# A hybrid encoder trunk in fp32 on one core: another order in the opening, in cross attention's second pair, and for the residual's transposes

## What is computed

```python
h = x + concat([y_a, y_b, y_c]) @ w_out
h = h + cross_attention(rmsnorm(h, norm_cross), rmsnorm(mem, norm_mem), wq, wkv, wo)

def cross_attention(u, m, wq, wkv, wo):          # 4 heads of 128
    q = (u @ wq).reshape(bsz, seq, 4, 128)
    kv = (m @ wkv).reshape(bsz, mlen, 2, 4, 128)
    k, v = kv[:, :, 0], kv[:, :, 1]
    s = einsum('bshd,bmhd->bhsm', q, k) * 128 ** -0.5
    p = softmax(s, axis=-1)
    o = einsum('bhsm,bmhd->bshd', p, v).reshape(bsz, seq, 512)
    return o @ wo
```

## Time and profile before

| | |
|---|---|
| time, median of 3 runs | 1197.31 us (1195.26, 1197.31, 1197.39) |
| profiled execution | 1195.13 us |
| its span (first to last instruction) | 1193.3 us, mean granted clock 0.997 |
| outside the span | 1.8 us |
| PE busy | 98% of the span |
| DVE, ACT busy | 75%, 55% |
| HBM | 181 GB/s over the span |

### The profile page before, as it was taken

The page is one execution under the profiler, slowest core; times in us unless marked ns, Lnnn a source line. Parts: engine busy times, 40 slices in busy tenths (PEclk is TensorE's granted clock), DMA queues, the critical chain, the costliest instruction groups (busy, mean ns, idle before and its releaser), DMA issues.

```text
span 1193.3 us, 18816 instructions
## 1 busy us (share of the span) xinstructions
PE 1171.8 (98%) x6956; PEld 1039.8 (87%) x6956; DVE 893.7 (75%) x1271; ACT 658.4 (55%) x870; POOL 0.2 (0%) x4
## 2 busy tenths in 40 slices
PE   8999999999999999999999999999999999999996
PEld 8899999999887978888888888888888888888885
DVE  6775999778866767877777777777677777777777
ACT  6555665566744557555455545454564645555455
POOL 0000000000000000000000000000000000000000
PEclk9999999999999999999999999999999999999999
DMA  9766656434556455675756657585766567575751
GB/s 352 215 162 177 177 142 177 133 108 141 200 194 180 155 164 139 204 212 176 210 177 195 192 164 199 167 222 185 195 192 189 176 195 192 174 211 176 212 176 71
DMA packets 303214, 217.11 MB, mean 182 GB/s; under 512 B 11350, under 2 KB 263998, under 8 KB 302526
## 3 DMA queue, kind: packets, MB, share of 16 engines
q1 hardware_dynamic: 302990, 216.31, 61.8%
q10 hardware_dynamic: 176, 0.14, 0.1%
HBM read 214.33 MB, written 2.10 MB: 181 GB/s over the span
## 4 chain that ended last, share of the span: by engine, by line
PE 86%; DVE 7%; issue 2%; ACT 1%; SPq 1%; DMA 1%; ACTq 0%; DVEq 0%
PE bank L1392 27%; PE bank L1396 14%; PE bank L1366 10%; PE bank L1367 9%; PE bank L1368 9%; PE bank L1369 4%; PE bank L1370 4%; PE bank L1371 4%; DVE lo L798 2%; DMA raw<-in_cross_wkv_dram 1%; PE bank L1464 1%; PE bank L1495 1%; ACT hi L388 1%; DVE arena L1000 1%; PE bank L1428 1%
## 5 line engine op out<-in xcount | busy, mean ns | idle before, releaser
L798 DVE TENSOR_TENSOR lo<-raw,hi 128x2048 fp32r<-128x2048 f32 x195 | 446.3, 2289 | 128.8 <-ACT hi L388 118.9
L388 ACT CAST hi<-raw 128x2048 fp32r<-128x2048 f32 x195 | 371.6, 1911 | 104.8 <-PE bank L1368 98.4
L1392 PE MATMUL bank<-ux,hi 128*128 128x512 f32 x1408 | 336.5, 391 | 0.0
L1392 PEld LDWEIGHTS bank<-ux,hi 128*128 128x128 f32 x1408 | 259.1, 188 | 50.6 <-DVE arena L1293 0.2
L1396 PEld LDWEIGHTS bank<-ux,lo 128*128 128x128 f32 x1408 | 180.9, 191 | 7.1
L1396 PE MATMUL bank<-ux,lo 128*128 128x256 f32 x1408 | 183.1, 283 | 0.0
L1366 PE MATMUL bank<-hi,ch 128*128 128x512 f32 x464 | 181.4, 391 | 1.4 <-DVE cl L1232 1.4
L1367 PE MATMUL bank<-lo,ch 128*128 128x512 f32 x464 | 180.3, 388 | 0.0
L1368 PE MATMUL bank<-hi,cl 128*128 128x512 f32 x464 | 180.2, 388 | 0.0
L1369 PE MATMUL bank<-ux,hi 128*128 128x256 f32 (+1 forms) x592 | 170.9, 289 | 0.0
L1371 PE MATMUL bank<-ux,lo 128*128 128x256 f32 (+1 forms) x592 | 168.1, 284 | 0.0
(11 more groups left out here) (247 smaller groups left out, 969.9 us busy)
## 6 DMA issues: line engine op xcount, KB each, us to landing
raw<-in_ffn_w_up_dram SPq DMA_DIRECT2D x88, 1024.0 KB, 5.8
raw<-in_ffn_w_down_dram SPq DMA_DIRECT2D x44, 1024.0 KB, 5.1
raw<-in_w_in_dram SPq DMA_DIRECT2D x28, 1024.0 KB, 5.6
raw<-in_w_out_dram SPq DMA_DIRECT2D x16, 1024.0 KB, 5.1
raw<-in_cross_wkv_dram SPq DMA_DIRECT2D x7, 1024.0 KB, 10.0
arena<-in_x_dram SPq DMA_DIRECT2D x4, 1024.0 KB, 8.2
raw<-in_cross_wq_dram SPq DMA_DIRECT2D x4, 1024.0 KB, 5.4
raw<-in_cross_wo_dram SPq DMA_DIRECT2D x4, 1024.0 KB, 5.1
```

The costliest lines, as they stand in the source:

```text
L388: a.mark(act.copy(hi[:, n % RING, :], raw[:, n % RING, :]), S("hi_ready"))
L798: d.mark(dve.tensor_tensor(lo[:, n % RING, :], raw[:, n % RING, :], hi[:, n % RING, :].bitcast(F32), ALU.subtract), S("lo_ready"))
L1392: pe.matmul(bank[b][:, :], hi[:, s, k * P:(k + 1) * P], ux[:, k, :, :].rearrange("p a b -> p (a b)"), start=(k == 0), stop=False)
```

## The change

It leaves the number of matmuls, transposes, copies, subtractions and DMAs as it is, and the order of the DMAs.

1. Opening, PE: the 48 matmuls of a quarter are no longer taken tile by tile in threes, but in passes over several tiles: first hi x `uh`, which waits only for `hi_ready` and `mem_hi`; later the passes that need a low part. Chunk 0 goes in two halves, and the transposes of quarter 1 lie between them; the transposes of quarters 2 and 3 lie behind the first pass of chunks 1 and 2. The same for the value products (`value_rows`): the 8 matmuls hi x `uh` wait for `hi_ready` alone.
2. Opening, ACT and DVE: group 0 of `mem` ahead of the first half of chunk 0, `split(1)` ahead of the groups 2 and 3, `split(4)` behind the squares of x, on ACT `split(5)` ahead of x's scaling, on DVE `split(5)` behind `key_taken`.
3. Output projection: the first 12 matmuls of chunk n + 1 go ahead of `turn_block`.
4. Cross attention: blocks 0 and 1 of `cross_wo` go both ahead of `turn_probs`, and the first two k tiles of block 2 (chunk `N_WO + 2`) around `head_out`: 4 matmuls before it, 8 behind it. So `split(N_WO + 2)` moves forward: on ACT ahead of the exponentials of the second pair, on DVE behind its divisions and ahead of `cross_lo(1)`.

```diff
@@ ACT
+            token_hi("mem", 0, V_MEM, mem_bank(0))
             act.wait_ge(S("first_landed").sem, 16)
             a.mark(act.copy(hi[:, 0, 0:CH // 2], raw[:, 0, 0:CH // 2]), S("first_hi"))
-            for g in (0, 1):
-                token_hi("mem", g, V_MEM, mem_bank(g))
+            token_hi("mem", 1, V_MEM, mem_bank(1))
             act.wait_ge(S("raw_landed0").sem, 16)
             a.mark(act.copy(hi[:, 0, CH // 2:], raw[:, 0, CH // 2:]), S("hi_ready"))
+            split(1)
             for g in (2, 3):
                 token_hi("mem", g, V_MEM, mem_bank(g))
-            split(1)
             split(2)
...
             split(3)
-            split(4)
             act.wait_ge(S("x_landed").sem, 32)
             a.settle()
             a.mark(act.activation(junk, xs[:, 0, :], ACT.Square, accum_out=small[:, s_ss:s_ss + 1]), S("x_ss"))
+            split(4)
             token_root("x")
+            split(5)
             act.wait_ge(S("x_r").sem, 1)
...
-            split(5)
...
             attend_out(A_X // 2)
+            split(N_WO + 2)
             attend_exp(A_X + 2)
@@ DVE (the same moves as ACT in the first quarters)
             split(3)
-            split(4)
             dve.wait_ge(S("x_landed").sem, 32)
             tile_squares("x", xs)
-            token_rsqrt("x", S("x_r"))
+            token_var("x")
+            split(4)
+            token_inverse("x", S("x_r"))
...
-            split(5)
             dve.wait_ge(S("products_done").sem, products(3))
             for j in range(X_H):
                 d.mark(dve.tensor_tensor(kxT[:, j, :], bank[j][:, 0:T], mem_scale, ALU.mult), S("key_taken"))
+            split(5)
...
             attend_norm(A_X + 3)
+            split(N_WO + 2)
             cross_lo(1)
@@ PE
+            def value_rows(n, g):
+                s = n % RING
+                pe.wait_ge(S("hi_ready").sem, n + 1)
+                for t in range(TT):
+                    for k in range(4):
+                        pe.matmul(bank[4 + t][:, :], uh[:, 4 * g + k, t * P:(t + 1) * P], hi[:, s, k * 512:(k + 1) * 512],
+                                  start=(g == 0 and k == 0), stop=False)
+                ready(n)
...
+            def key_products(q, ks, weights, tokens, lo_signal, start, stop):
+                for k in ks:
+                    kk_ = 4 * q + k
+                    if lo_signal and k % 2 == 0:
+                        pe.wait_ge(S(lo_signal).sem, 2 * (kk_ // 2) + 2)
+                    for j in range(X_H):
+                        o = k * 512 + j * P
+                        last = pe.matmul(bank[j][:, 0:T], weights[:, q % RING, o:o + P], tokens[:, kk_, :],
+                                         start=(start and kk_ == 0), stop=(stop and kk_ == KD - 1))
+                return last
...
             turn_mem(0)
+            pe.wait_ge(S("first_hi").sem, 1)
+            key_products(0, (0, 1), hi, uh, "mem_hi", True, False)
+            key_products(0, (0, 1), hi, ul, "mem_lo", False, False)
+            pe.wait_ge(S("first_lo").sem, 1)
+            key_products(0, (0, 1), lo, uh, None, False, False)
+            turn_mem(1)
+            pe.wait_ge(S("hi_ready").sem, 1)
+            key_products(0, (2, 3), hi, uh, "mem_hi", False, False)
+            key_products(0, (2, 3), hi, ul, "mem_lo", False, False)
+            ready(0)
+            key_products(0, (2, 3), lo, uh, None, False, False).then_inc(done, 1)
+            for q in range(1, 4):
+                pe.wait_ge(S("hi_ready").sem, q + 1)
+                key_products(q, range(4), hi, uh, "mem_hi", False, False)
                 if q < 3:
                     turn_mem(q + 1)
...
             for n in range(N_XV, N_XV + 4):
-                ready(n)
                 g = n - N_XV
-                row_product(n, uh, ul, 4 * g, 4, g == 0, g == 3)
+                value_rows(n, g)
...
                 row_product(n, uh, ul, 10, mla_b, True, False)
+                ready(n + 1)
+                row_product(n + 1, uh, ul, 14, mla_b, False, True, signal=False, ks=(0, 1))
                 if cb > 0:
                     turn_block("hx", "mix_added", cb - 1, 8 + 4 * cb, hx_bank)
-                ready(n + 1)
-                row_product(n + 1, uh, ul, 14, mla_b, False, True, signal=False, ks=(0, 1))
...
             row_product(N_WO, ch, cl, 0, 0, True, False, signal=False, ks=range(2))
+            ready(N_WO + 1)
+            pe.wait_ge(S("scores_taken").sem, A_X + 4)
+            row_product(N_WO + 1, ch, cl, 0, 2, True, False, signal=False, ks=range(2))
             both(turn_probs, A_X // 2 + 1)
-            ready(N_WO + 1)
-            row_product(N_WO + 1, ch, cl, 0, 2, True, False, signal=False, ks=range(2))
+            third = N_WO + 2
+            pe.wait_ge(S("hi_ready").sem, third + 1)
+            for k in (0, 1):
+                wh = hi[:, third % RING, k * 512:(k + 1) * 512]
+                pe.matmul(bank[4][:, :], ch[:, k, 0:P], wh, start=(k == 0), stop=False)
+                pe.matmul(bank[4][:, :], cl[:, k, 0:P], wh, start=False, stop=False)
             both(head_out, A_X // 2 + 1)
+            ready(third)
+            for k in (0, 1):
+                pe.matmul(bank[4][:, :], ch[:, k, 0:P], lo[:, third % RING, k * 512:(k + 1) * 512], start=False, stop=False)
+            for k in (0, 1):
+                three(bank[5][:, :], hi[:, third % RING, k * 512:(k + 1) * 512], lo[:, third % RING, k * 512:(k + 1) * 512],
+                      ch[:, k, P:T], cl[:, k, P:T], k == 0, False, stationary_x=True)
             pe.wait_ge(S("cross_lo").sem, 2)
```

More of the change, by code:

```diff
@@ L712, in _ @@
                 cb = n - N_WO
-                split(n + 2)
+                if cb >= 1:
+                    split(n + 2)
                 if cb >= 2:
@@ L812, in newton, with token_var, token_inverse @@
                 go(dve.tensor_tensor(r, r, t, ALU.mult), last)
+            def token_var(name):
+                go(dve.tensor_scalar(small[:, s_var:s_var + 2], small[:, s_ss:s_ss + 2], 1.0 / D, EPS, ALU.mult, ALU.add), S(f"{name}_var"))
             def token_rsqrt(name, last=None):
+                token_var(name)
+                token_inverse(name, last)
+            def token_inverse(name, last=None):
                 v, sd = small[:, s_var:s_var + 2], small[:, s_std:s_std + 2]
                 r, t_ = small[:, s_r:s_r + 2], small[:, s_t:s_t + 2]
-                go(dve.tensor_scalar(v, small[:, s_ss:s_ss + 2], 1.0 / D, EPS, ALU.mult, ALU.add), S(f"{name}_var"))
                 dve.wait_ge(S(f"{name}_std").sem, 1)
@@ L909, in _ @@
             dve.wait_ge(S("vecs_ready").sem, 1)
+            token_lo("mem", 0, V_MEM, mem_bank(0))
             dve.wait_ge(S("first_hi").sem, 1)
@@ L912, in _ @@
                    S("first_lo"))
-            for g in (0, 1):
-                token_lo("mem", g, V_MEM, mem_bank(g))
+            token_lo("mem", 1, V_MEM, mem_bank(1))
             dve.wait_ge(S("hi_ready").sem, 1)
@@ L1411, in row_product @@
                     last.then_inc(done, 1)
+            def value_rows(n, g):
[6 more added lines that the diff above has]
+                ready(n)
+                for t in range(TT):
+                    for k in range(4):
+                        pe.matmul(bank[4 + t][:, :], uh[:, 4 * g + k, t * P:(t + 1) * P], lo[:, s, k * 512:(k + 1) * 512],
+                                  start=False, stop=False)
+                        last = pe.matmul(bank[4 + t][:, :], ul[:, 4 * g + k, t * P:(t + 1) * P], hi[:, s, k * 512:(k + 1) * 512],
+                                         start=False, stop=(g == 3 and k == 3))
+                last.then_inc(done, 1)
             def turn_group(name, src, g, b):
@@ L1516, in turn_mem @@
                     turn_group("mem", mems, g, mem_bank(g))
-            turn_mem(0)
-            for q in range(4):
+            def key_products(q, ks, weights, tokens, lo_signal, start, stop):
[8 more added lines that the diff above has]
+                return last
@@ L1520, in _ @@
+            ready(0)
[3 more added lines that the diff above has]
+                key_products(q, range(4), hi, uh, "mem_hi", False, False)
                 if q < 3:
                     turn_mem(q + 1)
-                if q == 0:
-                    pe.wait_ge(S("first_lo").sem, 1)
+                if q < 3:
+                    ready(q)
+                    key_products(q, range(4), lo, uh, None, False, False)
+                    key_products(q, range(4), hi, ul, "mem_lo", False, False).then_inc(done, 1)
@@ L1524, in _ @@
                 else:
+                    key_products(q, range(4), hi, ul, "mem_lo", False, False)
                     ready(q)
[L1526 to L1540, removed]
@@ L1541, in _ @@
-                last.then_inc(done, 1)
+                    pe.wait_ge(S("vectors_landed").sem, N_VECTORS)
+                    for m, (r, col) in enumerate(((V_ROWS_A, 0), (40, V_CW), (88, V_FW), (88, V_FW + 88), (88, V_FW + 176), (88, V_FB))):
```

(5 more changed lines are left out.)

2 lines of the change are left out of this document (1 added, 1 removed).

## The result

| | before | changed |
|---|---|---|
| median | 1197.35 us (4 runs, 1195.26 to 1197.52) | 1186.08 us (4 runs, 1185.68 to 1186.71) |
| profiled execution | 1195.13 us, span 1193.3 | 1186.10 us, span 1184.1 |
| ratio | | 0.991, 95% interval 0.9893 to 0.9928 |

The changed kernel is 0.9% faster. The profiled executions differ by 9.0 us, the medians by 11.3. Three runs of the kernel before in the comparisons further down took 3005, 4137 and 6332 us; they are left out of all its figures.

What follows compares the result with a forecast made beforehand. PE, busy 98% of the span, was taken as the bound, with only its standing or half-clock time to win: 5.5 + 1.6 + 2.0 = 9.1 us off 1195.13 gives 1186.0, with 1.1 added 1187.0; range 1184.5 to 1191.0.

Steps and rivals of the forecast that it cites:

- opening: Up to x's first transposes: PE's wait for DVE's key tiles goes, start at 41.0 not 46.52, 5.5 us won.
- projection: Output projection: 12 matmuls cover the 0.54 us that PE loses three times, 1.6 us won.
- cross attention: Cross attention: PE's waits of 3.3 us go, PE arrives 3.0 earlier, waits 1.0 for DVE's low tiles; 2.0 us won.
- Chunk 3's copy: Opening, ACT: tightest operand of the key's products, copied by 28.5 us when PE wants it at 28.6.
- The margin: Opening, x's transposes: PE arrives at 41.0, 1.8 us behind all it needs; also the margin of a late x or chunk 4.
- the stretch at 11 to 14.6 us: Opening of the kernel before: the lower clock behind PE's idle time costs 1.50 us; full clock taken as likelier after.
- I add half: Sum: half of the 2.2 us by which the median lies above the profiled execution is added, 1186.0 to 1187.1.
- the stretch from block 1 to the end of `head_out`: Cross attention, PE: 8 transposes, 4 matmuls and `head_out`, from 427.95 to 431.7 us.
- Rival 1: Opening: the slow stretch stays, 4.0 us won for 5.5; 1187.5, or 1188.6 with the half; chance 0.25.
- Rival 2: Opening: chunk 3's copy or x's chain 2 to 3 us late; 1188.6, with the half 1189.7; chance 0.15.
- Rival 3: Cross attention and projection: PE's waits only move to the next semaphore; 1189.6, with the half 1190.7; chance 0.07.
- Rival 4: Opening: x lands d late, PE waits d - 1.8; slower than before if d is above 11 us; chance 0.02.

Runs made afterwards that it cites:

- e3: Kernel before with only the opening's product passes, `value_rows` and the new order of the first two chunks and groups 0 to 3: 1197.31 us, ratio 1.0000.
- e11: Changed kernel with the two loads of x issued behind that of chunk 4, so that x lands later: 1186.58 us, ratio 0.9916 to before.
- e6: Kernel before with 12 matmuls of zeros filling PE's first wait, for `mem`: 1197.78 us, ratio 1.0003.
- e2: Kernel before with only the cross attention part of the change: 1194.81 us, ratio 0.9974.
- e5: Kernel before with 11 matmuls of zeros while PE waits for DVE's key tiles: 1195.62 us, ratio 0.9985.
- e7: Changed kernel with DVE's low tiles of groups 2 and 3 ahead of the subtraction of FFN chunk 1: 1184.96 us, ratio 0.9896 to before.
- e1: Kernel before with only the output projection part of the change: 1195.20 us, ratio 0.9982.
- e12: Changed kernel without the product passes and the order of the first chunks and groups: 1188.28 us, ratio 0.9916 to before.
- e8: Changed kernel as it is, run again as a measure: 1186.15 us, ratio 0.9908 to before.
- e4: Kernel before with only the opening's new places for the splits of chunks 4 and 5 on ACT and DVE: 1192.56 us, ratio 0.9959.

## Why the prediction was right, and where not

**The sum** was 1186.0 for an execution like the profiled one; that was 1186.10, and the forecast of 1187.0 is 0.9 above the median. By parts, predicted and read from the starts in the two traces: opening 5.5 and 4.9; projection 1.6 and 1.8 (415.58 against 422.30 is 6.7, less 4.9); cross attention 2.0 and 2.5. That the total met the measured one within 0.1 us is partly luck: the opening gave 0.6 less than I said and the other two 0.7 more. The forecast's distance of 0.9 comes from the 1.1 that I added to the sum (see the clock).

**Opening.** The steps held but the start and one margin. I let PE begin at 8.8, from the copy's time in the profiled execution of before; it began at 9.21, as the transposes ahead came 0.4 later (6.63 against 6.20) and the copy now stands behind group 0, which needs them. The start of the transposes is a difference between executions (6.02 to 7.29 with the same warm-up); in e3's, where they started at 6.22, the products began at 8.81. From there 26.46 us to the key's end against my 26.3. Chunk 3's copy, the tight place, was over at 28.5 as laid out, and PE came no sooner than it. The margin was read wrongly: 1.8 us is that of the vectors' copy (39.2 against 41.0), while DVE's key tiles, from 38.4 on for 1.41, end at 39.8 by my own figures and leave 1.2. The changed trace has 2.2 and 1.6 for the two. e11 shows that it is there and how far it goes: 2.6 us of delay cost some 0.4.

**Clock.** That the stretch at 11 to 14.6 us took 1.50 us from the kernel before was right for those 48 matmuls and wrong for the kernel, in which the key wait stood behind it (e6, ratio 1.0003, and e2's trace); the sum did not use it, as it went by the starts of x's transposes. The term that failed is the 2.2 us between the median and the profiled execution, of which "I add half": 1.1 was added where nothing was to be added. By e3 and e5 it is the price of a slow stretch behind the key wait. The six traces of the changed opening (changed, e7 to e11) have no such wait and the clock at 1.00 from 10 to 60 us, and their runs lie within 1.1 us of each other in each comparison. This is why the medians gained 11.3 where the sum says 9.1. That most executions of before have the stretch is inferred from the times (15 of 21 above 1197 us beside e5), since its one trace has none there. The Trainium skill, "TensorE: Matmul & The Clock Gate", Part 1, has the point of the clock's change vary from run to run of one kernel. This case's traces agree: with the same opening, the granted clock behind the first wait fell to 0.50 in the executions of before (a wait of 2.9 us) and e1 (1.6), and stayed at 1.00 in e2's (2.0).

**Projection.** As laid out, and none of the three waits moved on. The 0.2 us more are 0.06 three times: eight transposes behind a wait held PE for 0.85 us (344.94 to 345.79) and without one for 0.79 (e1, 347.12 to 347.91).

**Cross attention.** The mechanism was right, DVE being late next (e7 removed that wait and won 1.2). The size was off by 0.5. Shifted by the 6.72 us won before, PE ended `head_out` at 431.28 where I had 431.7, and the low tiles were ready at 442.11 + 1.65 + 6.72 = 450.5 where I had 451.0. The term that was too large is the stretch from block 1 to the end of `head_out`: I allowed 3.75 us (427.95 to 431.7) for 8 transposes, 4 matmuls and `head_out`, and they took 3.34 (421.22 to 424.56). The chain on DVE starts from there, so these tenths came through.

**The rivals.** Rival 1 (slow stretch stays) did not happen in any trace of the changed kernel. Rival 2 did not either: chunk 3's copy and x's chain were in time in all of them. That a landing can shift by 1.2 us is seen in e6; what it would do to the changed opening is not tested. Rival 3 is refuted by e1 and e2. Rival 4's mechanism has about the margin that I gave it: PE's wait was to be d - 1.8, so 0.8 at d = 2.6, where e11 gives 0 to 0.5.

## What to carry to other kernels

Of two chains that meet at one wait, shortening one may measure as nothing (e3) and still be worth a microsecond or two once the other is short (e12 against e8), so halves of a change have to be tried together as well as alone. Where an engine's clock depends on its activity, a wait can cost its own length and in some executions a slow stretch behind it: look at the spread of the runs and at the granted clock behind each wait, and do not take a good profiled execution for the typical one. And for each stall that is removed, follow the next engine's work to the next wait; here that named both the 1.0 us that was not won and the exchange of instructions on DVE that won it (e7).

## What the runs showed of the hardware

- The granted clock fell to 0.50 behind waits of 5.5 us (e3), 3.5 (e2, the key wait), 3.0 and 2.9 (e4 and before, the first one), 1.7 (e6) and 1.6 (e1, the first one), and stayed at 1.00 behind 2.4 (before, the key wait), 2.0 (e2 and e12, the first one) and 1.5 (changed). The length of the wait alone does not tell which.
- With a wait of 2.4 us filled with matmuls of zeros the clock behind it was 1.00 in the profiled execution, and the kernel was some 2 us faster in the median (e5).
- The same 14 warm-up matmuls ended at different times: what follows them began at 6.02 to 7.29 us.
- One chunk of 1 MB, issued in the same order, was copied from 16.69 us on in one execution and from 17.87 on in another.
